# Scores three units ahead in a third PSUM bank for the last pair, and queries projected before the second group of keys

## What is computed

```
proj = x @ w_in                      # queries and keys of group A and B, values
oa = banded_attention(qa, ka, va, 128, slopes, 1.0, sink)       # group A: +-128 tokens, 8 heads
ob = dilated_attention(qb, kb, vb, slopes)                      # group B: (128,1), (512,4), (2048,16), 8 heads
mix = concatenate([rms_norm(oa), rms_norm(ob)], -1) @ w_out
x = layer_norm(ALPHA * x + mix)
```

## Time and profile before

| what | value |
|---|---|
| time, median of 3 runs | 1330.6 us (1330.6 to 1331.35) |
| the profiled execution's own time | 1325.05 us |
| its span, first to last instruction | 1323.2 us |
| mean granted TensorE clock | 0.973 |
| PE busy | 93% of the span |
| DVE, ACT, POOL busy | 55%, 45%, 15% |
| chain that ended last, by engine | PE 72%, DMA 7%, DVE 7%, issue 5% |
| first bias of pairs 0, 1, 2, 3 | 142.94, 274.35, 402.78, 530.50 us |
| last bias of pair 3 | 676.32 us |

### The profile page before, as it was taken

How to read it: one execution, slowest core, us unless ns; L and a number is a source line. 1 busy time by engine, 2 the same in 40 slices (tenths; PEclk the granted TensorE clock), 3 DMA queues, 4 the chain that set the end, 5 groups by cost and what they waited for, 6 DMA issues and landing times.

```text
span 1323.2 us, 21973 instructions
## 1 busy us (share of the span) xinstructions
PE 1235.7 (93%) x8066; PEld 1112.4 (84%) x8066; DVE 732.8 (55%) x1760; ACT 590.0 (45%) x1428; POOL 196.5 (15%) x244
## 2 busy tenths in 40 slices
PE   7999899999999999997799999998899999999993
PEld 6998788888788888886677888897889999999882
DVE  3110355654555455555768876458455565556358
ACT  3221334443444444444543332222365666566455
POOL 0000001200120021011111121001032333233212
PEclk9999999999999999998799999899999999999997
DMA  6534643373437343673354433514889999999773
GB/s 196 158 119 126 161 112 93 81 185 84 108 82 194 79 107 94 159 182 89 98 192 178 152 114 111 223 64 132 306 264 275 265 280 290 272 265 292 188 269 143
DMA packets 157906, 224.35 MB, mean 170 GB/s; under 512 B 40016, under 2 KB 109392, under 8 KB 157776
## 3 DMA queue, kind: packets, MB, share of 16 engines
q1 hardware_dynamic: 146064, 180.28, 45.8%
q0 software_dynamic: 9216, 33.56, 11.1%
q10 hardware_dynamic: 2544, 9.44, 1.8%
HBM read 141.15 MB, written 52.20 MB: 146 GB/s over the span
## 4 chain that ended last, share of the span: by engine, by line
PE 72%; DMA 7%; DVE 7%; issue 5%; SPq 3%; ACT 3%; POOL 1%; DVEq 1%; ACTq 0%; POOLq 0%
PE bank L800 16%; PE bank L802 16%; PE bank L801 16%; PE bank L907 8%; PE bank L794 5%; PE bank L894 4%; PE bank L883 3%; SPq L534 3%; PE bank L884 2%; DMA d_work<-in_w_up 2%; PE bank L1017 2%; DMA acc_scratch<-d_work,dstc 2%; DMA Q<-stage_lo 1%; DVE w_gu_lo L1782 1%; DVE d_work L1980 1%
## 5 line engine op out<-in xcount | busy, mean ns | idle before, releaser
L1262 ACT ACTIVATE b_work<-b_work 128x256 f32<-128x256 f32 (+3 forms) x288 | 148.1, 514 | 267.9 <-DVE b_work L1598 267.1
L800 PE MATMUL bank<-xgT_hi,w_gu_hi 128*128 128x256 f32 x704 | 202.4, 288 | 5.2 <-DVE xgT_lo L1659 2.9
L802 PE MATMUL bank<-xgT_hi,w_gu_lo 128*128 128x256 f32 x704 | 200.4, 285 | 0.0
L801 PE MATMUL bank<-xgT_lo,w_gu_hi 128*128 128x256 f32 x704 | 200.4, 285 | 0.0
L1607 DVE COPY b_work<-bank 128x256 f32<-128x256 f32 (+2 forms) x256 | 112.7, 440 | 118.7 <-PE bank L894 118.2
L800 PEld LDWEIGHTS bank<-xgT_hi,w_gu_hi 128*128 128x128 f32 x704 | 136.3, 194 | 10.7 <-issue 7.5
L2072 POOL CAST Q<-Q 128x512 fp32r<-128x512 f32 x48 | 53.4, 1145 | 595.1 <-DVE w_k_lo L1564 356.0
L801 PEld LDWEIGHTS bank<-xgT_lo,w_gu_hi 128*128 128x128 f32 x704 | 136.3, 194 | 0.1
L802 PEld LDWEIGHTS bank<-xgT_hi,w_gu_lo 128*128 128x128 f32 x704 | 136.2, 194 | 0.0
L894 PE MATMUL bank<-keep,b_work 128*128 128x128 f32 x608 | 117.2, 279 | 16.9 <-ACT b_work L1262 16.9
L894 PEld LDWEIGHTS bank<-keep,b_work 128*128 128x128 f32 x608 | 81.1, 141 | 53.7 <-ACT b_work L1262 23.4
(11 more groups left out here) (192 smaller groups left out, 2820.8 us busy)
## 6 DMA issues: line engine op xcount, KB each, us to landing
d_work<-in_w_gate SPq DMA_DIRECT2D x16, 1024.0 KB, 8.9
d_work<-in_w_up SPq DMA_DIRECT2D x16, 1024.0 KB, 11.4
d_work<-in_w_down SPq DMA_DIRECT2D x16, 1024.0 KB, 10.9
Q<-stage_hi SPq DMA_DIRECT2D x96, 128.0 KB, 2.4
Q<-stage_lo SPq DMA_DIRECT2D x96, 128.0 KB, 2.4
o_scratch<-b_work SPq DMA_DIRECT2D x36, 264.0 KB, 3.2
c_work<-o_scratch SPq DMA_DIRECT2D x12, 792.0 KB, 5.1
raw_w<-in_w_in SPq DMA_DIRECT2D x26, 256.0 KB, 4.2
```

The source lines that it names most:

```text
L800: nc.tensor.matmul(o, w_hi, x_hi, start=first, stop=False)
L801: nc.tensor.matmul(o, w_hi, x_lo, start=False, stop=False)
L802: return nc.tensor.matmul(o, w_lo, x_hi, start=False, stop=last)
L1262: nc.scalar.activation(prob[:, u % 2, 0:n], prob[:, u % 2, 0:n], ACT.Exp, scale=-1.0, bias=o[:, HD:HD + 1], accum_out=o[:, HD + 1:HD + 2])\
```

## The change

It does five things.

1. `PROJ` puts the queries `("q", 0, 1)` ahead of the keys `("k", 1)`. The ranges of steps change with it: 0 to 6, 8 to 13, 14 to 18, 19 to 24 in pairs 0 to 2; in the last pair 0 to 6, 8 to 13, 14 to 18, 19 to 23, 24 to 30, 32 to 46. The queries need the new `w_q`, whose split stays in step 7; now the group that uses it begins in step 8. SP's wait for `qk_made` 16 moves ahead of the second copy.
2. In pair 0, the stage copy of the first keys (`PRE - 1`) moves from step 0 to step 2 on ACT and DVE.
3. In the last pair, scores run three units ahead from unit 36 on: units 34 and later use banks 0, 1 and 7 in turn and three parts of `prob`, and step 33 begins two units.
4. Because bank 7 is taken, the first tile's transposes go through bank 6 in two halves (steps 55 and 57), and only eight parts of its output projection, steps 59 to 66, stand inside the loop. The other eight come behind it.
5. In the last pair SP loads the output weights after one group less is made, and sends the fifth projection ahead of `store_o(3)`.

```diff
-OP_UNIT = 58
-OP_UNITS = 12
+OP_UNIT = 59
+OP_UNITS = 8
...
-            prob = take(2, 384)
+            prob_all = take(2 * 384)
...
-        PROJ = [("q", 2, 0), ("k", 1, None), ("q", 0, 1), ("k", 2, None), ("q", 1, 0), ("q", 2, 1),
+        PROJ = [("q", 2, 0), ("q", 0, 1), ("k", 1, None), ("k", 2, None), ("q", 1, 0), ("q", 2, 1),
                 ("k", 0, None), ("q", 0, 0), ("q", 1, 1)]
...
-        PLAN = proj_plan([(0, 5), (6, 11), (12, 17), (18, 24), (25, 31), (33, 40), (41, 51), (52, 61), (62, 71)])
-        PLAN_LAST = proj_plan([(0, 5), (6, 10), (11, 16), (17, 24), (25, 33), (35, 46)])
+        PLAN = proj_plan([(0, 6), (8, 13), (14, 18), (19, 24), (25, 31), (33, 40), (41, 51), (52, 61), (62, 71)])
+        PLAN_LAST = proj_plan([(0, 6), (8, 13), (14, 18), (19, 23), (24, 30), (32, 46)])
...
-            return {end[0] + 2: 0} if last else {end[0] + 2: 0, end[3] + 2: 1, end[5] + 2: 2}
+            return {end[0] + 1: 0} if last else {end[0] + 1: 0, end[3] + 2: 1, end[5] + 2: 2}
+        THREE = 34
+        def begun(g, i, last):
+            if last and g == THREE - 1:
+                steps = (2, 3)
+            else:
+                steps = (3,) if last and g >= THREE else (2,)
+            return [at for at in (unit_at(g + d, i, last) for d in steps) if at is not None]
+        def score_at(u, last, n):
+            b = (0, 1, 7)[(u - THREE) % 3] if last and u >= THREE else u % 2
+            return bank[b][:, 0:n]
+        def prob_at(u, last, n):
+            c = 256 * ((u - THREE) % 3) if last and u >= THREE else 384 * (u % 2)
+            return prob_all[:, c:c + n]
...
+                wait("qk_made", i * UNITS + 16)
                 dup_pair(1, i)
                 store_o(1, i)
-                wait("qk_made", i * UNITS + 16)
                 dup_pair(2, i)
                 if last:
-                    sp.wait_ge(S["proj_made"], PRE + GROUPS * i + 3)
+                    sp.wait_ge(S["proj_made"], PRE + GROUPS * i + 2)
...
                 if last:
+                    dup_pair(4, i)
                     store_o(3, i)
-                    dup_pair(4, i)
...
+                if last and u == THREE + 2:
+                    pe.wait_ge(S["proj_ready"], GROUPS * i + PRE + 5)
...
-                        if n in (2, 6, 7):
-                            pe.wait_ge(S["wq_lo"], i * 6 + (8, 10, 12)[(2, 6, 7).index(n)])
+                        if n in (1, 6, 7):
+                            pe.wait_ge(S["wq_lo"], i * 6 + (8, 10, 12)[(1, 6, 7).index(n)])
...
+            def ot_half(h, sem):
+                for c in range(4):
+                    end = nc.tensor.transpose(bank[6][:, P * c:P * c + P],
+                                              om_of(0, 0)[:, 512 * h + P * c:512 * h + P * c + P], ident)
+                end.then_inc(sem, 1)
...
-            STAGE_FREE = [("dup_q", 2), ("dup_q", 3), ("dup_done", 5), ("dup_q", 4), ("dup_done", 6),
+            STAGE_FREE = [("dup_q", 2), ("dup_q", 3), ("dup_q", 4), ("dup_done", 5), ("dup_done", 6),
...
-                    if g == 0:
+                    if g == (0 if i else 2):
...
-                    if (at := unit_at(g + 2, i, last)) is not None:
+                    for at in begun(g, i, last):
```

More of the change, by code:

```diff
@@ L325, in encoder_layer @@
             od_ld0 od_ld1 xr_ld0 xr_ld1 x1_st0 x1_st1 op_made res_done oT_made oT_hi oT_lo om_ready
-            merge_need merge_exp merged squares rms_rstd ln_var ln_rstd x1_ready x1T_made x1T_ready
+            oT0_made oT0_hi oT0_lo merge_need merge_exp merged squares rms_rstd ln_var ln_rstd x1_ready x1T_made x1T_ready
             lg_made lg_ready lgexp_done
@@ L877, in qk @@
                 for c, keys in k:
-                    o = bank[u % 2][:, at:at + c]
+                    o = score_at(u, last, n)[:, at:at + c]
                     if kind == 1:
@@ L894, in pT @@
                     end = nc.tensor.transpose(bank[2 + u % 2][0:r, P * c:P * c + P],
-                                              prob[:, u % 2, at[c]:at[c] + r], ident)
+                                              prob_at(u, last, n)[:, at[c]:at[c] + r], ident)
                 end.then_inc(S["pT_made"], 1)
@@ L948, in pair @@
                         pe.wait_ge(S["proj_ready"], PRE + GROUPS * i + LAST_GROUPS)
-                        ot(0, 0, bank[6:8])
+                        pe.wait_ge(S["om_ready"], 1)
+                        ot_half(0, S["oT0_made"])
+                    if last and g == OT_UNIT + 2:
+                        pe.wait_ge(S["oT0_lo"], 1)
+                        ot_half(1, S["oT_made"])
                     if last and OP_UNIT <= g < OP_UNIT + OP_UNITS:
@@ L1261, in exps @@
                 n, o = kinds[u][5], ost[u // BLOCK % 3][:, u % 4, kinds[u][1], :]
-                nc.scalar.activation(prob[:, u % 2, 0:n], prob[:, u % 2, 0:n], ACT.Exp, scale=-1.0,
+                nc.scalar.activation(prob_at(u, last, n), prob_at(u, last, n), ACT.Exp, scale=-1.0,
                                      bias=o[:, HD:HD + 1], accum_out=o[:, HD + 1:HD + 2])\
@@ L1296, in pair @@
                     if last and g == OT_UNIT + 1:
-                        oT_high(0, 0, bank[6:8], oT0_hi)
+                        act.wait_ge(S["oT0_made"], 1)
+                        copy(oT0_hi[:, 0:512], bank[6][:]).then_inc(S["oT0_hi"], 1)
+                    if last and g == OT_UNIT + 3:
+                        act.wait_ge(S["oT_made"], 1)
+                        copy(oT0_hi[:, 512:1024], bank[6][:]).then_inc(S["oT_hi"], 1)
                     for t, m in enumerate(MERGES if last else ()):
@@ L1597, in bias @@
                 dve.wait_ge(S["qk_made"], i * UNITS + u + 1)
-                V.tensor_tensor_reduce(out=prob[:, u % 2, 0:n], in0=bank[u % 2][:, 0:n], in1=tab,
+                V.tensor_tensor_reduce(out=prob_at(u, last, n), in0=score_at(u, last, n), in1=tab,
                                        scale=-(HD ** -0.5), scalar=BIG, op0=ALU.add, op1=ALU.min,
@@ L1637, in pair @@
                     if last and g == OT_UNIT + 1:
-                        oT_low(0, 0, bank[6:8], oT0_hi, oT0_lo)
+                        dve.wait_ge(S["oT0_hi"], 1)
+                        V.tensor_tensor(oT0_lo[:, 0:512], bank[6][:], plain(oT0_hi[:, 0:512]), ALU.subtract)\
+                         .then_inc(S["oT0_lo"], 1)
+                    if last and g == OT_UNIT + 3:
+                        dve.wait_ge(S["oT_hi"], 1)
+                        V.tensor_tensor(oT0_lo[:, 512:1024], bank[6][:], plain(oT0_hi[:, 512:1024]), ALU.subtract)\
+                         .then_inc(S["oT_lo"], 1)
                     for t, m in enumerate(MERGES if last else ()):
```

## The result

| kernel | median, us | runs | ratio to before, 95% interval |
|---|---|---|---|
| before | 1330.47 | 20 | |
| the change | 1333.91 | 20 | 1.0031 [1.0017, 1.0046] |

The change makes the kernel 4.1 us slower (2.3 to 6.1 by the interval), a little more than what counts as no change here. The prediction was 1332.9 us, +2.3, with the chances split almost evenly between no change and slower.

What follows compares the result with a forecast made beforehand. PE, busy 93% of the span, was taken to bound pairs 0 to 2, ACT and DVE in turn the last pair from 608 us; -12.3 + 8.0 + 3.0 + 3.6 = +2.3 us gave 1332.9 us, range 1324 to 1338.

Steps and rivals of the forecast that it cites:

- Start of pair 0: Units 2 to 5: stage copy in step 2 saves 4.24 us, 2.60 of PE waiting and 1.64 of slow clock.
- Before unit 24: Pairs 0 to 2: earlier queries remove PE's waits of 2.41, 1.60 and 2.49 us, 6.50 us in all.
- Step 8: All four pairs: PE waits 2.0 us for the w_q subtractions, 8.0 us added; bounds 1.2 to 2.6 per wait.
- slow stretch: Matmuls at lower clock after a wait, 1.6 us each; one in two step 8 waits, 3 us added (0 to 6).
- The ring: Last pair, w_o steps: bias, exponential, ACT's w_o high part, DVE's w_o subtraction, next bias; stays 2.38 us with three units ahead.
- The rule of the Trainium skill: Rival, last pair: third score bank fills PE's 10.7 us of waits for exponentials, giving 1321.2 us; chance 0.06.
- Four parts behind the loop: Four output projection parts ahead of tile 0's residual: 2.7 us, about 0.5 hidden by a load wait, so +2.2 us.
- The halves: First tile's transposes in two halves: same work for DVE and ACT in two places, costing nothing.
- Queries of unit 40: Last pair: they come 0.4 us later (1.7 earlier to 0.5 later); stall stays but divided, PE also waiting in step 32.
- The sum: Whole kernel: -12.3 + 8.0 + 3.0 + 3.6 = +2.3 us, giving 1332.9 us.
- the third bank's: Last pair, three units ahead: 2.4 us lost at unit 40, 1.4 won by the bank, net 1.0 us more.
- the 1.6 us that I took away for pair 1: Before unit 24: 1.6 us saved for the slow stretch after the 1.60 us wait, priced like pair 0's.

Runs made afterwards that it cites:

- e3: The change with its first group of projections in steps 0 to 5, so w_q is split in step 6 instead of 7: 1323.46 us, -6.4 against before.
- e6: Kernel before, two units ahead, with first tile's transposes in halves through bank 6 and eight output projection parts inside the loop: 1335.34 us, +6.4 against before.
- e2: Kernel before with three units ahead, third bank, halves, eight parts inside the loop and two last-pair ranges ending earlier; old projection order: 1334.93 us, +5.9 against before.
- e7: Kernel before with VectorE's low part of each w_o piece one step after ScalarE's high part: 1320.24 us, -7.6 against before.
- e8: e2 (three units ahead, third bank, old projection order) with the low parts of w_o one step later: 1322.40 us, -5.6 against before.
- e11: The whole change with the early split (e3) and the low parts of w_o one step later (e7): 1312.66 us, -18.1 against before.
- e9: Kernel before with one number changed, eight instead of twelve parts of the first tile's output projection inside the loop: 1334.23 us, +5.2 against before.
- e10: e5 and e7 in one kernel, two units ahead: reordering, early split, stage copy in step 2, w_o low later: 1310.60 us, -19.3 against before.
- e5: e1 with its first group of projections in steps 0 to 5 and the split of w_q in step 6: 1320.99 us, -7.0 against before.
- e1: The change without third bank, halves and eight parts: only new projection order, stage copy in step 2 and SP's order: 1329.41 us, -0.1 against before.
- e4: Kernel before with only the stage copy of pair 0's first keys moved from step 0 to step 2: 1325.27 us, -5.1 against before.

## Why the prediction was right, and where it was not

**Start of pair 0, -4.2 us: right.** 6.27 us as forecast; alone it measured -5.1.

**Before unit 24, -6.5 us: right**, no wait left in pairs 0 to 2.

**Step 8, 2.0 us four times: right.** It measured 1.87. PE came to its wait 2.4 us after the last part and not 2.3, VectorE was done after 4.15 and not 4.3, because neighbouring instructions overlap by 0.08 us and the sum laid them end to end; PE began 0.15 us behind that. Two of four slow, as priced. With both gone (e3) 10.5 us came back, where the two terms say 8 + 3 = 11. The price of a slow stretch holds too: pair 1, where the clock stayed up, is 1.3 us longer in the change than in e3, pairs 0 and 2 are 2.8 longer, so 1.4 us for a stretch that was priced at 1.6. Pairs 0 to 2, first bias to first bias, went from 387.6 to 384.1 us: -3.4, where the terms give -12.3 + 6 + 2.3 = -4.0. In e3, without the waits, they are 10.3 us shorter than in the profile of before, against the 12.3 of the prediction; 0.8 of the difference are the two waits for `w_q_lo` that e3 still has there.

**The ring, no gain from three ahead: right.** 2.38 us stayed, e6 and e2 put the bank at -0.5 us where the terms said +1.0, and e7 shows by cutting it that the ring held the pace of these steps: 1.34 us instead of 2.38 where nothing else is due. The rule of the Trainium skill against it, "Perfetto Trace Analysis", section "Optimization Strategy", that the same gap repeating on the busiest engine can mean too few buffers, would have given 1321 us. It does not hold for this kernel as it stands; in e8 and e11, where the ring is cut, the bank does shorten the last pair.

**Four parts behind the loop, +2.2 us: mis-sized.** It measured 5.2 (2.8 to 7.6). The step that failed is the price at PE's full clock. The parts themselves took 2.7 us and 0.6 was hidden, about as forecast; 2.9 us more came with the clock behind the loop. The clock was priced for the waits in step 8 and not for the steps that the parts used to fill.

**The halves "cost DVE and ACT the same work in two places; nothing": wrong in its place, open in the total.** The steps around them took 3 us or more longer in the profile of e6 than with whole transposes; in the median e6 less e9 is 1.2 us, within the uncertainty. The prediction looked at the work and not at PE, which now waits 2.6 us for the first half's copy, with a low clock around it.

**Queries of unit 40, +0.4 us: place right, size too low.** The stall moved to step 32, as forecast, and is as long as before (3.40 us and 3.53). But the term asked only when the copies land. It left out the projection parts that the new ranges put ahead of unit 40, and e10 and e5 reach its bias 2.8 to 5.0 us later than the five kernels with the old ranges. The medians ask for less: e1 measured -0.1 where the other terms give -12.3 + 8 + 3 = -1.3, which leaves 1.2 us for it, give or take 2.

**The sum.** Terms +2.3, measured +4.1. What the prediction said of pairs 0 to 2 and of the ring is borne out piece by piece. In the last pair three terms were too low (the four parts by 3.0 us, the queries of unit 40, the halves), and the third bank's was 1.5 too high. That the total came out 1.8 us from the forecast is therefore partly luck. The two profiles can't close the account: they are 14.7 us apart where the medians are 3.4.

## What to carry to other kernels

When a kernel that ran in balance gets a new order, look for the first use that lost its cover: here a subtraction that had sat behind matmuls became four waits of 1.87 us, and one step's shift of its producer took them back. A deeper buffer won nothing here while the steps ran in a ring through another engine; letting the consumer in the ring take its input one step later won 7.6 us. Work that stood in idle time inside the loop was free there; put behind it, it cost nearly its full duration and as much again in slow matmuls.

## What the runs showed of the hardware that I had not expected

Which waits are followed by slow matmuls looked like a coin in one profile, and like a pattern over many. Windows right behind the wait before unit 24, in pairs 0, 1 and 2 of e2 (the granted clock is the third number from the end):

```profile
199.00:203.00 4.00, 4.00 (x20) 3.52 (x20) 1.24 (x6) 0.96 (x3) 0.00 (x0) 0.61 0.00 0
326.00:330.00 4.00, 4.00 (x28) 3.61 (x29) 1.90 (x8) 1.54 (x5) 0.00 (x0) 1.00 0.00 0
455.00:459.00 4.00, 4.00 (x22) 3.64 (x21) 1.23 (x5) 0.97 (x4) 0.00 (x0) 0.61 0.00 0
```

The same two of three, pairs 0 and 2, were slow in the profiles of e4, e7, e8 and e9; in that of before it was pair 1 alone, in e6 pair 2 alone. Behind the new waits it was again pairs 0 and 2 of four, in the change and in e1. So before's profiled execution had less of it than most, and the 1.6 us that I took away for pair 1 may stand for twice as much in a median run.
